# Step-size and decay projection spread by token tile between three convolution products, and twelve identity products ahead of the last turn of the differential mixer

## What is computed

```python
# first block, layer 1: the differential mixer
p  = masked_softmax(logits, dist >= 0)              # 8 heads, two maps each
pd = p[:, :, 0] - lam_full * p[:, :, 1]
o  = jnp.einsum('bhqs,bshe->bqhe', pd, v)
o  = rms_norm(o, subln) * (1.0 - lambda_init)       # then @ w_out
...
# second block: 16 meta tokens are put ahead, so 272 tokens
u = rms_norm_2(h, norm_mix_pre[l])
dq, dk, dv, dz, db, da, aq, ak, av = jnp.split(u @ w_in[l], split_points, axis=-1)
# dq, dk, dv go through a short convolution; db, da (8 columns each) give
beta = jax.nn.sigmoid(db)
g = -jnp.exp(a_log) * jax.nn.softplus(da + dt_bias)  # step size and decay of the delta rule
```

## The kernel before

| bank | last used for | released by |
|---|---|---|
| 4 | values of pair 1 | DVE, `pair_normed` of pair 1 |
| 6 | turn of head 6 | ACT, `pT` of head 6 |
| 7 | values of pair 2 | DVE, `pair_normed` of pair 2 |
| 5 | turn of pair 1 | DVE, low part of pair 1 |

## Time and profile before

### The profile page before, as it was taken

The page is one execution under the profiler, slowest core; times in us unless marked ns, Lnnn a source line. Parts: engine busy times, 40 slices in busy tenths (PEclk is TensorE's granted clock), DMA queues, the critical chain, the costliest instruction groups (busy, mean ns, idle before and its releaser), DMA issues.

```text
span 1132.3 us, 19834 instructions
## 1 busy us (share of the span) xinstructions
PE 1077.2 (95%) x8085; PEld 957.7 (85%) x8085; DVE 751.0 (66%) x1258; ACT 607.1 (54%) x1094; POOL 94.4 (8%) x120
## 2 busy tenths in 40 slices
PE   6999989999999999999999999999779999999997
PEld 4989567989899899878898988999668878898986
DVE  1786887898997865568855447787476657444443
ACT  2544755554454556647445465547765436555453
POOL 0012770000000000000000000032420000000000
PEclk9999999999999999999999999999689999999999
DMA  9997116799998455433955653260000145555541
GB/s 374 420 401 324 39 38 260 288 351 368 343 342 297 150 186 187 150 130 135 351 188 188 226 182 110 76 242 19 2 2 21 50 156 186 187 186 186 190 146 38
DMA packets 33563, 218.27 MB, mean 193 GB/s; under 512 B 4529, under 2 KB 5297, under 8 KB 8897
## 3 DMA queue, kind: packets, MB, share of 16 engines
q1 hardware_dynamic: 33472, 217.00, 51.9%
HBM read 215.93 MB, written 1.05 MB: 192 GB/s over the span
## 4 chain that ended last, share of the span: by engine, by line
PE 79%; DVE 9%; ACT 7%; DMA 2%; issue 2%; POOL 1%; DVEq 0%; SPq 0%; ACTq 0%; POOLq 0%
PE bank L527 21%; PE bank L529 20%; PE bank L528 20%; ACT high L515 2%; DVE low L521 2%; DMA ring<-ada_halves 2%; PE bank L567 1%; PE bank L644 1%; PE bank L2484 1%; DVE y_tmp L1607 1%; PE bank L1149 1%; DVE stats L1609 1%; DVE y_tmp L1596 1%; ACT zb L1134 1%; DMA ring<-raw_ksv 1%
## 5 line engine op out<-in xcount | busy, mean ns | idle before, releaser
L521 DVE TENSOR_TENSOR low<-ring,high 128x2048 fp32r<-128x2048 f32 (+1 forms) x139 | 317.7, 2288 | 234.8 <-ACT high L515 234.3
L515 ACT ACTIVATE high<-ring 128x2048 fp32r<-128x2048 f32 (+1 forms) x139 | 264.7, 1906 | 245.4 <-PE bank L529 183.8
L527 PE MATMUL bank<-act_high,high 128*128 128x256 f32 (+1 forms) x1072 | 308.9, 288 | 0.0
L529 PE MATMUL bank<-act_high,low 128*128 128x256 f32 (+1 forms) x1072 | 304.2, 284 | 0.0
L528 PE MATMUL bank<-act_low,high 128*128 128x256 f32 (+1 forms) x1072 | 304.2, 284 | 0.0
L527 PE MATMUL bank<-high,act_high 128*128 128x512 f32 (+1 forms) x632 | 233.8, 370 | 3.2 <-DVE act_low L3078 1.8
L528 PE MATMUL bank<-low,act_high 128*128 128x512 f32 (+1 forms) x632 | 231.2, 366 | 0.0
L529 PE MATMUL bank<-high,act_low 128*128 128x512 f32 (+1 forms) x632 | 231.1, 366 | 0.0
L527 PEld LDWEIGHTS bank<-act_high,high 128*128 128x128 f32 x1072 | 205.4, 192 | 4.5 <-issue 2.4
L528 PEld LDWEIGHTS bank<-act_low,high 128*128 128x128 f32 x1072 | 205.6, 192 | 2.4 <-issue 1.4
L529 PEld LDWEIGHTS bank<-act_high,low 128*128 128x128 f32 x1072 | 205.5, 192 | 0.0
(11 more groups left out here) (512 smaller groups left out, 1347.9 us busy)
## 6 DMA issues: line engine op xcount, KB each, us to landing
ring<-chunks SPq DMA_DIRECT2D x138, 1024.0 KB, 5.1
ring<-ada_halves SPq DMA_DIRECT2D x38, 1024.0 KB, 6.3
o_land<-ada_halves SPq DMA_DIRECT2D x6, 1024.0 KB, 11.6
ring<-raw_cmp SPq DMA_DIRECT2D x4, 1024.0 KB, 11.4
x_tok<-ada_halves SPq DMA_DIRECT2D x3, 1024.0 KB, 14.9
gate_rows<-ada_b SPq DMA_DIRECT2D x4, 512.0 KB, 10.1
bias<-bias_by_distance SPq DMA_DIRECT2D x1, 2048.0 KB, 13.4
ln_rows<-ln_g SPq DMA_DIRECT2D x4, 512.0 KB, 5.9
```

The lines of the kernel that those rows point to most:

```text
L515: e.activation(weights(c)[0], in_ring(("w", c)), ACT.Copy).then_inc(*act.up("high", c))
L521: e.tensor_tensor(low, in_ring(("w", c)), high.bitcast(F32), ALU.subtract).then_inc(*vec.up("low", c))
L527: e.matmul(out_, ah, bh, start=start, stop=False)
L529: return e.matmul(out_, al, bh, start=False, stop=stop)
```

## The change

Two things, both on PE alone. In `diff_tensor`, step 9, twelve identity products stand ahead of the turn of head 7. In `in_tensor`, the `ba` products are cut by token tile: tile 0 goes behind the third convolution product, tile 1 behind the fourth, tile 2 behind the fifth. The signal that `ba` is made comes with tile 2.

```diff
             for step in range(STEPS):
                 h = step - 2
+                if h == 7:
+                    keep_running(e, 12, "diff")
                 if 0 <= h < 8:
                     unit_turn_tensor(e, D0 + 2 * h, vec)
...
-            for n, i0 in enumerate((4, 6, 0, 2)):
+            for n, i0 in enumerate((4, 6, 0, 2, 8, 10)):
                 conv_product(e, IN2 + n, i0)
-            b = ps.take(e, "ba", vec, "ba")
-            w_ = in_ring(("raw", "ba"))
-            e.wait_ge(*ring_landed(("raw", "ba")))
-            for t in range(3):
-                r = TT_ROWS[t]
-                m = token_product(e, w_, 0, 16, u2T, rows_of(t), b[0:r, t * 16:t * 16 + 16])
-            m.then_inc(*pe.up("raw", "ba"))
-            for n, i0 in enumerate((8, 10)):
-                conv_product(e, IN2 + 4 + n, i0)
+                t = n - 2
+                if t == 0:
+                    b, w_ = ps.take(e, "ba", vec, "ba"), in_ring(("raw", "ba"))
+                    e.wait_ge(*ring_landed(("raw", "ba")))
+                if 0 <= t < 3:
+                    r = TT_ROWS[t]
+                    m = token_product(e, w_, 0, 16, u2T, rows_of(t), b[0:r, t * 16:t * 16 + 16])
+                    if t == 2:
+                        m.then_inc(*pe.up("raw", "ba"))
```

## The result

| | before | changed |
|---|---|---|
| median, us | 1135.83 (7 runs) | 1143.11 (7 runs) |
| lowest and highest | 1133.00, 1140.45 | 1141.56, 1145.98 |
| profiled execution | 1134.16 | 1143.11 |
| its span | 1132.3 | 1141.3 |

The ratio is 1.0058, with a 95% interval of 1.0044 to 1.0071: the changed kernel is slower by 6.6 us (5.0 to 8.1); the two medians lie 7.3 us apart. The forecast was +7.8 us, 1144.8, with a range of 1140.0 to 1147.8. The median of before has moved by 1.2 us since the forecast, as more runs were added.

The account below looks back on a forecast made before the run. PE was taken to bound the kernel, busy 95% of the span. Step 9's +3.2 us and the second block's +4.6 us made +7.8 us, on a median of 1137.0 us giving 1144.8 us, range 1140.0 to 1147.8.

Parts of the forecast that it names:

- Filling: Step 9: the identity products take 2.7 us, fill PE's 2.47 us idle gap and delay head 7's turn by 0.1 us.
- The bank: Step 9: head 6's values get the bank where pair 2 still awaits scaling, so PE starts them 3.2 us later.
- The clock in part one: Step 9: after 3.1 us idle the dip to 1.2 GHz returns some 3 us later, so nothing is won.
- I take the value of the nearer row: Step 9 clock: expect a dip as after 2.47 us idle, not full speed as after 1.10 us.
- the 3.2 us that I gave as the most: Two clock dips, step 9 and `ba`, about 1.6 us each: the most the change could bring, 0.3% of the time.
- The gain of the spread: Second block: spreading `ba` avoids the dip, so PE finishes the sixth convolution product 1.3 us earlier.
- The reload: Second block: IN2+6, issued 6.0 us later, lands 6.0 us after issue; PE idles 4.4 us, `akv` is 3.1 us late.
- The clock in part two: Second block: 4.4 us of idleness brings a dip in the `akv` products, 1.5 us (bounds 0 and 1.7).
- The sum: Whole kernel: 3.2 us from step 9 plus 4.6 us from the second block, +7.8 us.
- The reload is covered: Rival, second block: slot released earlier or piece needed later; that half gains 1.3 us, whole +1.9, 1138.9; chance 0.07.
- the bank is free: Rival, step 9: pair 2 scaled before head 6's values are due; whole +3.1 us, 1140.1; chance 0.06.
- Faster: Rival, both places: clock stays at 2.4 GHz and neither wait is felt; -2.8 us, 1134.2; chance 0.04.

Follow-up runs that it names:

- e1: Twelve identity products in a bank of their own in step 9, projection unchanged, against the kernel before: 1.0029, +3.3 us.
- e2: Only the `ba` projection spread by token tile as in the change, no identity products, against the kernel before: 1.0027, +3.1 us.
- e4: Changed kernel without identity products, `ba` tiles one convolution product earlier; ratio to the kernel before 1.0015.
- e5: e3 and e4 together: identity products in the turn's own bank and the earlier spread, against the kernel before: 0.9998.
- e9: e4 run once more: projection spread one convolution product earlier, no identity products, against the kernel before: 1.0007.
- e8: The kernel before, unchanged, profiled a second time: 1133.24 us, one run.
- e7: As e1 but one identity product instead of twelve, in a bank of its own, against the kernel before: 1.0046, +5.2 us.
- e3: Twelve identity products in step 9 written into the bank that head 7's turn takes anyway, against the kernel before: 0.9991.
- e10: e3 run once more: twelve identity products in the bank of head 7's turn, against the kernel before: 0.9988.
- e6: Kernel before with one wait added on SP, issuing piece IN2+6 only after the fifth convolution product; PE's program untouched: 1.0056, +6.4 us.

## Why the prediction was right, and where it was off

*Filling.* Right: the turn started 2.68 us after the first of the 12 products, for a forecast of 2.7, and without a gap behind them.

*The bank.* Right: PE idle 2.90 us, released by the scaling of pair 2, and the whole of it passed on. Against undipped step 9 (23.41) the changed kernel's 26.74 is +3.3 us, forecast 3.2; with a dip in both, e1's 28.29 against 25.00 is +3.3 as well.

*The clock in part one.* The dip was forecast to come back on the same products. In the changed kernel's profile it did not, but stood in the norm behind; in e1 it stood in both places. The step "I take the value of the nearer row" took one execution's dip for a property of the code. In the six profiles whose step 9 is that of before it stands in four; in the seven whose `ba` group is, in three. So, as an estimate from these few profiles, the identity products have some two thirds of 1.6 us to win, about 1.0, and the spreading three sevenths of 1.1, about 0.5, not the 3.2 us that I gave as the most. None of the three profiles with the filling in the turn's bank has a dip in step 9.

*The gain of the spread.* Forecast 1.3 us. As forecast, no profile with the spread projection (the changed kernel, e2, e4, e5, e9) has a dip around the `ba` products. The gain holds against an execution with the dip (41.77 against 40.73 in e4 is 1.0), and is nothing against one without (40.65).

*The reload.* The mechanism was right and each step of the chain was seen: issue later by 6.0 us against the first convolution product, ACT waiting for the transfer, PE for DVE. The mis-sized term is the landing: 6.0 us taken from the same burst, 4.8 measured, so PE's idle time was 2.85 us for a forecast of 4.4, and the lateness against before 1.8 us, under even the bound of 2.1, for 3.1. Against the undipped 40.65 us it is 2.9. The other 0.3 us of the idle time is the sixth convolution product, which ended that much later behind the issue than reckoned. The 6.0 us, too, were the value of one execution: where the issue stands as in before, the same piece took 6.0, 5.9, 6.1, 5.0, 5.1 and 5.2 us to land (before, e8, e7, e1, e3, e10). In the late versions it took 4.8, 5.0 and 4.9 (changed, e2, e6); whether a late issue always lands this fast is not shown. The Trainium skill's "DMA: Bandwidth & Descriptors", by its split of fixed and variable cost, gave an estimate of 4.4 us; the measured 4.8 is nearer to it than my 6.0, and, like every landing of such a piece shown here, above it. The page fits that split to transfers of the GpSimd path, and these pieces are issued by SP, which the prediction did not say.

*The clock in part two.* Forecast 1.5 us; 2.8 in the changed kernel, where PE was slow for 6.1 us from `akv` on, and 1.4 in e2. Here the error went the other way: 1.3 us too much for the lateness, most of it the landing, and 1.3 too little for the clock in this profile. So the 1.8 + 2.8 = 4.6 us that the two stretches lost are the forecast's 4.6 by luck.

*The sum.* 7.8 against 6.6 measured. The landing's 1.2 us are as large as the difference, but in the changed kernel's own profile they were made up by the clock, and the clock's part over many executions is argued from few profiles, not shown. The two waits, the sign and their places were foreseen; how near the total came is partly luck.

*The rivals.* "The reload is covered" and "the bank is free" are what e4 and e3 build on purpose, and they took away the loss of their half. "Faster" was thought at -2.8 us; e5, which has neither wait, measured 0.9998, so that number was wrong too. It counted two dips that are often not there; whether that is all of it stays open, as e5 says above.

## What to carry to other kernels

Where banks or buffers are handed out as a queue, an added taker moves everyone behind it by one: list who releases the next three entries and when, before adding a harmless filler, or let the filler write into the bank that its successor takes anyway. Where a slot is refilled by a transfer, the last reader's place in the order is the transfer's issue time, so moving a cheap reader back by 6 us can cost a wait that has nothing to do with its own 4 us. And a clock dip in one profile is one draw: look at the same place in the profiles of other versions before counting it as a gain.

## What the runs showed of the hardware

The same code met the low clock in one execution and not in another. Step 9's idle time of 2.47 us was followed by granted clock 0.51, one of 2.34 us in unchanged code by 1.00, and one of 2.44 us by a dip in e2 and by none in e6; the `ba` group was followed by 0.50 in the first profile of before and by 1.00 in the second. Behind 2.90 us of idleness the clock stayed up in the changed kernel and fell in e1. The stretch from the first delta product to the end, which no experiment touches, took between 356.2 and 363.4 us. The shortest have no dip between 845 and 1120 us, and the longest (e4) has one of 13.7 and one of 3.4 us there. This alone is as wide as most effects here, and it is what a version worth 1 us has to be measured against. The landing of one 1024 KB piece at the head of the same burst varied as well, from 5.0 to 6.2 us where it was not issued late.
